# Splitting the norms ahead of an attention block's projections into halves of the tokens, in a two-block transformer kernel on one Trainium2 core

## What is computed

```python
x = _residual(x, _swiglu(_modnorm(x, g[0], m[0], m[1]), ffn1_w1[l], ffn1_w3[l], ffn1_w2[l]),
              g[1], m[2], HALF_STEP)
h_ctx = _residual(h_ctx, _swiglu(_modnorm(h_ctx, g[0], mc[0], mc[1]), ffn1_w1[l], ffn1_w3[l], ffn1_w2[l]),
                  g[1], mc[2], HALF_STEP)
pw = (w_in[l], b_gate[l], g_q_lora[l], g_kv_lora[l], w_uq[l], w_ukv[l])
qa, ka, va, qn, qr, kn, kr, vb, ga, gb = _project(_modnorm(x, g[2], m[3], m[4]), *pw)
cqa, cka, cva, cqn, cqr, ckn, ckr, cvb, cga, cgb = _project(_modnorm(h_ctx, g[2], mc[3], mc[4]), *pw)
```

## Time and profile before

| what | value |
|---|---|
| time, median of 3 runs | 2806.02 us (2804.84 to 2806.3) |
| the profiled execution: its own time | 2802.78 us |
| its span | 2801.0 us |
| mean granted clock of TensorE over the span | 0.994 |
| busy: PE, DVE, POOL, ACT | 98%, 48%, 28%, 18% |

### The profile page before, as it was taken

How to read it: one execution, slowest core, us unless ns; L and a number is a source line. 1 busy time by engine, 2 the same in 40 slices (tenths; PEclk the granted TensorE clock), 3 DMA queues, 4 the chain that set the end, 5 groups by cost and what they waited for, 6 DMA issues and landing times.

```text
span 2801.0 us, 29331 instructions
## 1 busy us (share of the span) xinstructions
PE 2742.1 (98%) x11634; PEld 1972.4 (70%) x11634; DVE 1356.6 (48%) x2497; ACT 493.3 (18%) x1077; POOL 796.0 (28%) x668
## 2 busy tenths in 40 slices
PE   8999999999999999999999999999999999999997
PEld 3655555555886378857888886775568858888873
DVE  7657565567237664325332336216573226544433
ACT  2100000003117262113000102005530000000011
POOL 1234343332223103411444430110034412444420
PEclk9999999999999999999999999999999999999998
DMA  6334333323200102221222221221012222222211
GB/s 252 119 109 133 103 116 120 94 83 117 81 32 10 62 1 69 90 90 56 80 91 90 91 75 60 76 78 46 31 46 90 91 83 76 91 86 80 90 62 58
DMA packets 51751, 231.63 MB, mean 83 GB/s; under 512 B 4256, under 2 KB 10784, under 8 KB 38176
## 3 DMA queue, kind: packets, MB, share of 16 engines
q1 hardware_dynamic: 40960, 181.17, 18.7%
q0 software_dynamic: 9072, 39.85, 4.4%
q10 hardware_dynamic: 1584, 8.75, 0.8%
HBM read 227.66 MB, written 2.10 MB: 82 GB/s over the span
## 4 chain that ended last, share of the span: by engine, by line
PE 60%; DVE 1%; ACT 0%; issue 0%; DVEq 0%; ACTq 0%
PE banks L657 40%; PE banks L593 15%; PE banks L1259 1%; PE banks L1178 1%; PE banks L1196 1%; PE banks L602 1%; PE banks L767 0%; PE banks L1261 0%; PE banks L1253 0%; DVE rstd L1856 0%; PE banks L1267 0%; PE banks L609 0%; DVE normed L1859 0%; DVE rstd L1871 0%; ACT scratch_a L1366 0%
## 5 line engine op out<-in xcount | busy, mean ns | idle before, releaser
L657 PE MATMUL banks<-big 128*128 128x256 f32 (+1 forms) x2240 | 572.2, 403 | 0.0
L2644 POOL TENSOR_TENSOR big<-weight_ring 128x512 f32<-128x512 f32 (+2 forms) x117 | 140.7, 1202 | 1353.7 <-PE banks L657 740.9
L657 PEld LDWEIGHTS banks<-big 128*128 128x128 f32 x2240 | 424.9, 190 | 112.8 <-DVE rpb_rows L1975 2.5
L657 PE MATMUL banks<-big,weight_ring 128*128 128x256 f32 (+1 forms) x1504 | 398.2, 409 | 3.3 <-DVE scratch_a L1981 2.6
L657 PEld LDWEIGHTS banks<-big,weight_ring 128*128 128x128 f32 x1504 | 285.3, 190 | 87.8 <-DVE scratch_a L1981 3.8
L657 PE MATMUL banks<-normed,weight_ring 128*128 128x256 f32 (+1 forms) x1312 | 342.5, 404 | 1.7 <-issue 0.9
L593 PE MATMUL banks<-normed,weight_ring 128*128 128x256 f32 (+2 forms) x912 | 298.2, 484 | 1.2 <-ACT normed L1384 0.6
L657 PEld LDWEIGHTS banks<-normed,weight_ring 128*128 128x128 f32 x1312 | 249.1, 190 | 69.2 <-issue 2.2
L593 PEld LDWEIGHTS banks<-normed,weight_ring 128*128 128x128 f32 (+1 forms) x912 | 168.0, 188 | 110.2 <-issue 94.5
L2645 POOL TENSOR_TENSOR big<-weight_ring 128x512 f32<-128x512 f32 (+2 forms) x142 | 211.6, 1490 | 0.0
L657 PE MATMUL banks<-normed,big 128*128 128x256 f32 (+1 forms) x840 | 203.7, 389 | 0.0
(11 more groups left out here) (448 smaller groups left out, 3348.0 us busy)
## 6 DMA issues: line engine op xcount, KB each, us to landing
weight_ring<-weights SPq DMA_DIRECT2D x144, 1024.0 KB, 4.8
rpb_rows<-w_ada POOLq DMA_DIRECT2D x28, 512.0 KB, 3.9
p_embed<-w_ada POOLq DMA_DIRECT2D x28, 512.0 KB, 3.8
weight_ring<-weights SPq DMA_DIRECT2D x16, 768.0 KB, 4.3
weight_ring<-weights SPq DMA_DIRECT2D x14, 512.0 KB, 3.3
weight_ring<-weights SPq DMA_DIRECT2D x8, 640.0 KB, 3.7
big<-w_ada POOLq DMA_DIRECT2D x2, 2048.0 KB, 8.4
residual<-xT ACTq DMA_DIRECT2D x2, 1536.0 KB, 12.2
```

The costliest lines, as they stand in the source:

```text
L657: last = nc.tensor.matmul(z, stationary(p), moving(p), start=opens and p == 0, stop=p == kp - 1, skip_group_check=True)
L2644: T(w[2], a11, a21, ALU.subtract).then_inc(sums_c, 1)
```

## The change

The latents' norms are made half by half: `nas` are two stages of 256 tokens each, with the contexts as a third (`na_context`). PE's four query tiles no longer run one after the other: for each half, for each k, all four tiles take that k. The square sums of the second half stand between k = 5 and k = 6 of the first half, those of the contexts at the same place of the second half. `turn_over` before the first sums goes from 13 to 8 matmuls, the one behind them from 12 to 6, and one of 128 columns is added between the sums of the first half. On GpSimd the sums of unit V_FFN1 no longer wait for the constants, inputs and bias rows; those of the next unit, V_FFN1 + 1, wait for one more product than ffn1 has.

```diff
@@ TensorE @@
-            turn_over(13, cst, 0, 2 * P)
-            norm_sums(na, LAT)
-            turn_over(12, cst, 0, 2 * P)
-            for b in range(4):
-                if b == 2:
-                    norm_sums(na_context, CONTEXT, (5,))
...
+            turn_over(8, cst, 0, 2 * P)
+            norm_sums(nas[0], HALVES[0:1], (5,), cst)
+            turn_over(6, cst, 0, 2 * P)
+            n = PROJ[0]
+            begin(n)
+            begin(n + 1)
+            for i, (x, y, _) in enumerate(HALVES):
                 for k in range(KC):
+                    if k == 6:
+                        norm_sums(*((nas[1], HALVES[1:2], (5,)) if i == 0 else (na_context, CONTEXT, (5,))))
+                    pe.wait_ge(na["ready"], i * KC + k + 1)
+                    for b in range(4):
+                        last = mm(bank[:, Q_BANK[b], x:y], slot(n + b // 2, (b % 2 * KC + k) * P, P), H[:, k, x:y],
+                                  k == 0, k == KC - 1, (i, k, b) in ((0, 0, 0), (1, KC - 1, 2)))
@@ ScalarE @@
-            root(na, LAT, (6,), na["y_root"], D)
+            halves_root(6, na["y_root"])
             act.wait_ge(sq1["used"], 2)
             root(na, CONTEXT, (7,), na["y_root"], D)
-            norm_squares(na, LAT)
-            norm(na, LAT, 3)
+            for g, half in zip(nas, HALVES):
+                norm_squares(g, [half])
+                norm(g, [half], 3, (5,))
@@ VectorE @@
-            for g, parts in ((na, LAT), (na_context, CONTEXT)):
-                post_norm(g, parts, GATE1)
-                norm(g, parts, modulated(SCALE2), True)
-            dve.wait_ge(na["ready"], KC)
-            dve.wait_ge(na["scaled"], 2 * KC)
+            post_norm(nas[0], HALVES[0:1], GATE1)
+            post_root(nas[1], HALVES[1:2])
+            norm(nas[0], HALVES[0:1], modulated(SCALE2), True)
+            post_add(nas[1], HALVES[1:2], GATE1)
+            post_root(na_context, CONTEXT)
+            norm(nas[1], HALVES[1:2], modulated(SCALE2), True)
+            post_add(na_context, CONTEXT, GATE1)
+            norm(na_context, CONTEXT, modulated(SCALE2), True)
+            dve.wait_ge(na["ready"], 2 * KC)
+            dve.wait_ge(na["scaled"], 3 * KC)
             row_sums_of(8, H, lambda i: [(0, 2), (2, 2)] if i in (1, 3) else [(0, 4)], (2, 0, 1, 3))
@@ GpSimd @@
+            pool.wait_ge(prod, 7 * V_FFN1)
+            weight_sums(V_FFN1)
+            pool.wait_ge(prod, 7 * V_FFN1 + 1)
+            for v in range(V_FFN1 + 1, V_LATER):
+                weight_sums(v)
             pool.wait_ge(inputs_landed, 16 * N_LOADS)
             pool.wait_ge(rpb_landed, 16)
             pool.wait_ge(consts_landed, 16)
-            pool.wait_ge(prod, 7 * V_FFN1)
-            for v in range(V_FFN1, V_LATER):
-                weight_sums(v)
```

More of the change, by code:

```diff
@@ L432, in build @@
         na, nb = (st(f"norm_{n}", "y_root", "xnew", "sq", "sq_used", "root", "scaled", "ready") for n in ("a", "b"))
-        na_context = dict(na, base=KC, turn=1)
+        nas = [dict(na, base=i * KC, turn=i) for i in range(2)]
+        na_context = dict(na, base=2 * KC, turn=2)
         nbs = [dict(nb, base=i * KC, turn=i) for i in range(2)]
@@ L855, in _ @@
             squares_of_both(sq1)
-            turn_over(13, cst, 0, 2 * P)
-            norm_sums(na, LAT)
-            turn_over(12, cst, 0, 2 * P)
-            for b in range(4):
-                if b == 2:
-                    norm_sums(na_context, CONTEXT, (5,))
-                n = PROJ[b // 2]
-                if b % 2 == 0:
-                    begin(n)
-                for k in range(KC):
[L868 to L872, removed]
+            turn_over(8, cst, 0, 2 * P)
[5 more added lines that the diff above has]
+            for i, (x, y, _) in enumerate(HALVES):
+                for k in range(KC):
+                    if k == 6:
[4 more added lines that the diff above has]
+                                  k == 0, k == KC - 1, (i, k, b) in ((0, 0, 0), (1, KC - 1, 2)))
+                        if i == 1 and k == KC - 1 and b != 2:
+                            last.then_inc(proj["done"], 2 if b == 3 else 1)
             def contexts(b, v):
@@ L877, in contexts @@
                 else:
-                    pe.wait_ge(na["ready"], 2 * KC)
+                    pe.wait_ge(na["ready"], 3 * KC)
                 for w in range(2):
@@ L888, in _ @@
                 if b == PROJ_FAST[0]:
-                    pe.wait_ge(na["root"], 2)
+                    pe.wait_ge(na["root"], 3)
                 if b == PROJ_FAST[1]:
```

## The result

| | median us (runs) | lowest to highest |
|---|---|---|
| before | 2806.66 (12) | 2804.05 to 2807.03 |
| changed | 2811.64 (12) | 2809.38 to 2814.82 |

The changed kernel is 5.0 us slower, a ratio of 1.002 with a 95% interval of 1.0013 to 1.0028, which is 3.6 to 7.9 us.

What follows compares the result with a forecast made beforehand. PE was taken as the bound, busy 98%, but made to wait for VectorE's row sums: second product +1.5 us, clock +2.8, together +4.3, or 2810.3 us on the median of 2806.02. Range 2803 to 2813.5.

Steps and rivals of the forecast that it cites:

- step 4: Latents' first half: reciprocal 1.79, one STT 0.52, shift and hand-over 0.6 put the first query matmul at 667.0.
- Step 1: Start of the norms: VectorE starts at 653.77 as before, still waiting for the tokens.
- The end of ffn1 beside GpSimd: First unit's sums moved to about 647.3 meet a VectorE add and delay the chain: +0.4 us, bounds 0 and 0.9.
- step 5: PE's first-half queries, then second half's sums, 4.4 us; k = 6 and 7 end at 685.25, H ready 685.2, just fitting.
- PE's first fast product and the stall: PE's first fast product ends at 705.3, then PE stalls for row sums until 715.2.
- Row sums beside GpSimd: Second unit's four GpSimd ops fall into VectorE's row sums: +4.0 us, between 3.3 and 4.3; 9 us instead of 5.
- The 5.1 us of the estimate: Row sums' growth if four whole GpSimd ops of 1.27 are added instead of turns, by the skill page's port lock.
- Second product: First fast unit's second product starts at 715.25 against 713.72: +1.5 us.
- Clock: The longer stall brings TensorE's lower clock onto dense products when PE returns: +2.8 us, bounds 0 and 3.4.
- the one in which the two don't meet: Row sums escape GpSimd's ops: second product at 711.25, stall 5.9 us, time about 2805, 2803.5 to 2806.5; chance 0.22.
- The faster rival: Row sums don't hold PE, which goes straight on from 705.3: -8.4 + 0.4, 2798; chance 0.06.
- The slower rival: Low clock holds 10 us of dense work, or ffn1's end loses the full 0.9: +6 to +8, 2813; chance 0.22.

Runs made afterwards that it cites:

- e5: Changed kernel without its GpSimd part, so only the norms in halves: 2811.01 us, +3.8 against before on the same chip.
- e1: Changed kernel with GpSimd's second-unit weight sums waiting for the second product of the first fast unit: 2806.79 us, +1.2 against before.
- e3: Changed kernel with 20 unread matmuls of 256 columns filling PE's stall between the first and second fast product: 2808.60 us, +3.0 against before.
- e9: Changed kernel without the new wait on GpSimd, second unit's sums running once their weights land: 2806.56 us, +1.0 against before.
- e7: Changed kernel with the context's square sums at k = 3 and GpSimd's second-unit sums behind the second product: 2798.97 us, -8.2 against before.
- e2: Kernel before plus the change's whole GpSimd part alone, both units' sums moved: 2801.53 us, -4.1 against before.
- e8: Kernel before with only the first unit's GpSimd sums moved to the end of ffn1: 2801.45 us, -5.7 against before.
- e4: Changed kernel with the context's square sums between k = 3 and k = 4 of the second half: 2803.47 us, -2.1 against before.
- e6: Changed kernel with the context's square sums at k = 4 and GpSimd's second-unit sums behind the second product: 2802.43 us, -4.8 against before.

## Why the prediction was right

**The sign and the mechanism held, and so did the size, in part by luck.** Forecast +4.3, measured +5.0 (3.6 to 7.9), by the marks +5.3. The time, 2811.64, is just above the 2808.5 to 2811.5 that I gave a chance of 0.5, and inside the whole range. The forecast has 0.4 us for the end of ffn1, ahead of the turn-over. The marks start at the turn-over and leave it out, so in their terms I forecast 1.1 up to the second product and 2.8 for the clock, +3.9, against +5.3. Step by step, from the turn-over:

- *First query matmul.* Forecast 13.5 us behind it (step 4), measured 13.7. Step 1 has VectorE wait for the tokens, as before; in the changed kernel its wait of 1.05 us is put down to ScalarE's root instead, and it starts 0.17 us behind the start of the turn-over, where it was 0.31. Hardly anything hangs on it.
- *The end of ffn1 beside GpSimd.* Taken as +0.4. PE's wait for the last square is 1.23 instead of the 1.02 that e5, without the move, still has: +0.2. One add took 0.77 for 0.56. The upper bound of 0.9 was far off.
- *Square sums beside queries.* Taken as 4.4 us each (step 5), measured 4.66 (679.30 to 683.96). This is just what the context's sums took before, from their start to the next row's (693.60 to 698.26); the 4.4 between that and PE's own 3.45 was a guess. The second half's query matmuls also have gaps of 0.4 us in them (14.27 for work of 13.85), since its H is just not there in time; step 5 had called this a fit. This is most of what was too small: together 0.9 us, and with the 0.2 of the first query matmul 1.1, by the start of the row sums.
- *PE's first fast product and the stall.* The part on the clock has the stall from 705.3 to 715.2, which counts the 0.4 at one end only; with it at both ends the forecast is 9.5 us. Measured 9.63: PE and VectorE are both about 1 us later than forecast.
- *Row sums beside GpSimd.* Forecast 9.0 us, measured 8.96; e1 shows it by itself, 5.03 without. The Trainium skill, "SBUF — State Buffer", section on its two sides, describes a lock for a whole instruction; the trace agrees that the two alternate instruction by instruction, and VectorE gets a turn after each GpSimd op. The 5.1 us of the estimate that used that page and four whole ops were too much; 3.95 were measured.
- *Second product.* Forecast +1.1 from the turn-over (+1.5 with the 0.4), measured +2.3.
- *Clock.* Forecast +2.8, measured +3.0 as the time from mark to mark, and 2.9 taken back by e3. That a stall brings the lower level was right; the size is partly luck. I had carried over 5.6 us of low clock behind PE's return, out of a stretch of 6.8. The stretch in the changed kernel was 10.2 us long (713.4 to 723.6), beyond that bound, and 4.3 of it fell on the stall, which left 5.9. After stalls of 5.67 and 5.68 us the cost was 1.7 in e9, 2.3 in e5 and 2.9 in e1.

Of the rivals, the one in which the two don't meet is e1 made real: it forecast -2.5 to +0.3; e1 measured +1.2, by the marks +1.3, with the second product 1.6 us earlier than before and 2.9 of clock behind it. It is 1 us above that range, which is about what the steps up to the row sums were too small by. The faster rival needed row sums that end before PE; e7 comes near to that (a stall of 0.49) with sums taken three k earlier, and gives -6.8 by the marks, where the rival had -8.0. The slower rival, a low clock that stays for 10 us of work, did not come: the low stretch was that long, but 5.9 us of it fell on work.

So the change is two parts that pull apart. The first unit's move is worth -4 us on the kernel before (e2, e8). The norms in halves and this move together bring the queries 12.6 us forward (3.9 by the move alone, e2; 7.2 by the halves alone, e5). With the context's sums at k = 6 they then leave PE waiting for the context: +1.2 and +1.0 us in e1 and e9, no gain, and some 5 us worse than the move alone. The new wait adds 4 us to that, as the row sums of e1 show. With the context's sums at k = 3, the halves are worth 2.9 us beyond e2 by the marks.

## What to carry to other kernels

When work is pulled forward on the engine that bounds, look for the next thing that it waits for and lay both ends out in one table: here 12.6 us were won at one wait and 14.9 lost by the second product (12.6 + 2.3) at the next, since a short chain on another engine started from a place far back in the first one's order. Where that chain's source stands in the order decides more than how early the whole begins; three k of queries moved from ahead of it to behind it turned +1.3 us into -6.8 by the marks (e1, e7). And a wait that moves GpSimd's work should be aimed at a stretch in which VectorE has slack (e8, e9) or reads PSUM, not at the signal that happens to come first. In the changed kernel VectorE's adds of 384 elements with an operand in PSUM kept their 0.55 us beside GpSimd (at 649.06 and 650.33), while the one between them with both operands in SBUF took 0.77 for 0.56.

## What the runs showed of the hardware

- GpSimd and VectorE alternate on SBUF operands, for VectorE's ops from 16 to 1024 elements: a coefficient op of 16 elements a partition took 1.12 us beside GpSimd at the end of ffn1 in e2, where its like take 0.17; and GpSimd's op of 512 elements was stretched to 2.24 us beside row sums of 1024. It is not strictly one for one: between two GpSimd ops there, two more coefficient ops ran at their 0.16 each, and the next took 1.24.
- A stall of PE of 4.23 us or more between dense matmuls was followed by the lower clock (changed, e1, e4, e5, e9), one of 2.22 us was not (e6). The low stretch overlapped work for long enough to cost 1.7 (e9) to 3.0 us (changed). How much of it falls on work differed from run to run, with the same stall too (e1 and e9). A shorter wait was followed by it where the work around it was broken: 3.19 us before, and 1.97 and 1.61 us between single square sums in e5.
- The lower clock also comes at places far from the change, and not in the same ones in each execution: the changed kernel's profile has a mean of 0.91 from 960 to 980 and 0.89 from 1900 to 1930, where the kernel before has 1.00 in both. The first 60 us show it best, ahead of the place of every edit: from 10 to 20 and from 30 to 60 the mean clock is 0.66 and 1.00 in the profiles of before, e2, e4, e6 and e8, and 0.83 and 0.94 in the other seven, and ffn1 ends 1.3 to 1.9 us later in these seven. I read this as a part of the scatter of 2 to 6 us between runs of one kernel; I did not test it.
